# A fused decoder block on one core: the moving operand of the 512 column products read as two interleaved runs, and the banks emptied in steps of two

## What is computed

```python
proj = x @ w_in                      # (1024, 1024) @ (1024, 6656)
q, k, v, cb, cc, ch, g_conv, g_attn = split(proj)
y_conv = cb * causal_conv3(cc * ch)
y_attn = sliding_window_attention(q, k, v, sinks)     # window 128, 16 query heads, 4 kv heads, ALiBi
merged = sigmoid(g_conv) * y_conv + sigmoid(g_attn) * y_attn
x = layer_norm(ALPHA * x + merged @ w_out, ln1)
hid = silu(x @ w_gate) * (x @ w_up)                   # 1024 -> 2816
x = layer_norm(ALPHA * x + hid @ w_down, ln2)
```

## Time and profile before

| | |
|---|---|
| median of 3 runs | 1456.26 us (1455.56 to 1458.51) |
| profiled execution, its own time | 1455.48 us |
| its span, first to last instruction | 1453.6 us |
| TensorE busy | 1436.0 us, 99% |
| VectorE busy | 796.9 us, 55% |
| GpSimd busy | 601.7 us, 41% |
| ScalarE busy | 485.3 us, 33% |
| mean granted TensorE clock | 0.998 |

### The profile page before, as it was taken

How to read it: one execution, slowest core, us unless ns; L and a number is a source line. 1 busy time by engine, 2 the same in 40 slices (tenths; PEclk the granted TensorE clock), 3 DMA queues, 4 the chain that set the end, 5 groups by cost and what they waited for, 6 DMA issues and landing times. The chain is left out here.

```text
span 1453.6 us, 19033 instructions
## 1 busy us (share of the span) xinstructions
PE 1436.0 (99%) x6658; PEld 1193.9 (82%) x6658; DVE 796.9 (55%) x1196; ACT 485.3 (33%) x933; POOL 601.7 (41%) x374
## 2 busy tenths in 40 slices
PE   9999999999999999999999999999999999999997
PEld 8888888888888888887887788888888888888886
DVE  3126664566357743767867835535345453454547
ACT  4433433333234423434245332322323223232133
POOL 2212122212212131124873483754737547464464
PEclk9999999999999999999999999999999999999999
DMA  5211111111111011111420121112111112121112
GB/s 174 59 44 44 41 33 55 32 43 43 43 43 43 29 44 46 41 44 59 121 83 15 58 74 44 58 44 65 51 42 58 51 58 65 29 64 59 44 51 116
DMA packets 128406, 80.22 MB, mean 55 GB/s; under 512 B 8432, under 2 KB 123120, under 8 KB 128368
## 3 DMA queue, kind: packets, MB, share of 16 engines
q1 hardware_dynamic: 128368, 79.73, 18.2%
HBM read 75.53 MB, written 4.19 MB: 55 GB/s over the span
## 5 line engine op out<-in xcount | busy, mean ns | idle before, releaser
L476 POOL TENSOR_TENSOR w_lo<-raw,w_hi 128x1024 fp32r<-128x1024 f32 x54 | 131.7, 2439 | 507.2 <-ACT w_hi L616 507.2
L1353 PE MATMUL ps<-act_hi,w_hi 128*128 128x512 f32 x864 | 338.6, 392 | 1.2 <-DVE act_lo L913 1.2
L1355 PE MATMUL ps<-act_hi,w_lo 128*128 128x512 f32 x864 | 336.6, 390 | 0.0
L1354 PE MATMUL ps<-act_lo,w_hi 128*128 128x512 f32 x864 | 336.5, 390 | 0.0
L564 POOL TENSOR_TENSOR w_lo<-raw,w_hi 128x512 fp32r<-128x512 f32 x80 | 108.5, 1356 | 227.7 <-ACT w_hi L826 227.7
L1355 PEld LDWEIGHTS ps<-act_hi,w_lo 128*128 128x128 f32 x864 | 162.2, 188 | 34.4
L1353 PEld LDWEIGHTS ps<-act_hi,w_hi 128*128 128x128 f32 x864 | 162.3, 188 | 33.5 <-issue 1.4
L1354 PEld LDWEIGHTS ps<-act_lo,w_hi 128*128 128x128 f32 x864 | 162.4, 188 | 32.0
L1353 PE MATMUL ps<-hid_hi,wd_hi 128*128 128x512 f32 x320 | 124.9, 390 | 3.4 <-DVE res L1192 3.4
L1198 DVE TENSOR_TENSOR res<-res,ps 128x512 f32<-128x512 f32 x128 | 87.9, 687 | 68.3 <-PE ps L1355 67.7
L1354 PE MATMUL ps<-hid_lo,wd_hi 128*128 128x512 f32 x320 | 124.5, 389 | 0.0
(11 more groups left out here) (193 smaller groups left out, 2548.0 us busy)
## 6 DMA issues: line engine op xcount, KB each, us to landing
raw<-in_w_in SPq DMA_DIRECT2D x52, 512.0 KB, 3.8
raw_d<-in_w_down SPq DMA_DIRECT2D x22, 512.0 KB, 3.3
raw<-in_w_gate SPq DMA_DIRECT2D x40, 256.0 KB, 2.9
raw<-in_w_up SPq DMA_DIRECT2D x40, 256.0 KB, 3.2
raw<-in_w_out SPq DMA_DIRECT2D x16, 512.0 KB, 3.6
xs<-in_x SPq DMA_DIRECT2D x8, 512.0 KB, 8.1
out<-rows SPq DMA_DIRECT2D x7, 512.0 KB, 2.6
raw_b<-in_w_gate SPq DMA_DIRECT2D x1, 512.0 KB, 5.3
```

Source lines behind the costliest of these rows:

```text
L476: pool.tensor_tensor(w_lo[:, slot], raw[:, slot], fp(w_hi[:, slot]), ALU.subtract).then_inc(w_lo_s, 1)
L1353: pe.matmul(bank, w_h(t), a_hi(t), start=(t == 0), stop=False)
L1354: pe.matmul(bank, w_h(t), a_lo(t), start=False, stop=False)
L1355: last = pe.matmul(bank, w_l(t), a_hi(t), start=False, stop=(t == tiles - 1))
```

## The change

Each product over half a tile of tokens now reads its moving operand through `folded`: element 0, element 256, element 1, element 257, and so on. That holds for the three matmuls of `product`, the three of `pair_product` and the product with v. The matmul still writes its bank in one run, so column 2b + a of the bank now belongs to token 256a + b. Whoever empties the bank reads it through `bank_of`: every second column (0, 2, 4, ...) for the first 256 tokens, then 1, 3, 5, ... for the others. The SBUF side of these instructions keeps its layout, and `tokens` only writes it as two runs of 256 so that shapes match. For the product with v, `o_ps` and `lo` are read in steps of two in the same way. No instruction is added, removed or moved on any engine, no semaphore and no transfer changes. The scores, transposes, statistics, last rows and all weight loads keep their patterns.

```diff
+        def folded(ap):
+            return ap.rearrange("p (a b) -> p b a", a=2)
+        def tokens(ap):
+            return ap.rearrange("p (a b) -> p a b", a=2)
+        def bank_of(b):
+            return ps[:, b, :].rearrange("p (b a) -> p a b", a=2)
...
-                        bank = ps[:, unit_bank(n), :]
+                        bank = bank_of(unit_bank(n))
...
-                            act.activation(tga[:, j, half(h)], bank, ACT.Tanh, scale=0.5).then_inc(ga_s, 1)
+                            act.activation(tokens(tga[:, j, half(h)]), bank, ACT.Tanh, scale=0.5).then_inc(ga_s, 1)
...
-                    o_ps = ps[0:HD, OUT, :].rearrange("p (j e q) -> p e j q", j=2, e=2)
-                    lo = o_lo[:].rearrange("p (j e q) -> p e j q", j=2, e=2)
+                    o_ps = ps[0:HD, OUT, :].rearrange("p (e q j) -> p e j q", j=2, e=2)
+                    lo = o_lo[:].rearrange("p (e q j) -> p e j q", j=2, e=2)
...
-                tile = res[:, m, half(h)]
+                tile, bank = tokens(res[:, m, half(h)]), bank_of(4 + v % 4)
...
-                    dve.tensor_tensor(tile, tile, ps[:, 4 + v % 4, :], ALU.add).then_inc(add_s, 1)
+                    dve.tensor_tensor(tile, tile, bank, ALU.add).then_inc(add_s, 1)
...
-                    pe.matmul(bank, w_h(t), a_hi(t), start=(t == 0), stop=False)
-                    pe.matmul(bank, w_h(t), a_lo(t), start=False, stop=False)
-                    last = pe.matmul(bank, w_l(t), a_hi(t), start=False, stop=(t == tiles - 1))
+                    hi, lo = folded(a_hi(t)), folded(a_lo(t))
+                    pe.matmul(bank, w_h(t), hi, start=(t == 0), stop=False)
+                    pe.matmul(bank, w_h(t), lo, start=False, stop=False)
+                    last = pe.matmul(bank, w_l(t), hi, start=False, stop=(t == tiles - 1))
...
-                                last = pe.matmul(ps[:, OUT, :], vs[:, n - 1 + kb, :], part[:, kb],
+                                last = pe.matmul(ps[:, OUT, :], vs[:, n - 1 + kb, :], folded(part[:, kb]),
...
-                    b_hi, b_lo = right(j, t)
+                    b_hi, b_lo = (folded(ap) for ap in right(j, t))
```

More of the change, by code:

```diff
@@ L631, in _ @@
                 act.wait_ge(unit_s, n + 1)
-                bank = ps[:, unit_bank(n + 1), :]
+                bank = bank_of(unit_bank(n + 1))
                 if t < 2:
@@ L635, in _ @@
                         act.wait_ge(v_turned, n - 1)
-                    act.activation(yc[:, half(n % 2)], bank, ACT.Copy).then_inc(v_copied, 1)
+                    act.activation(tokens(yc[:, half(n % 2)]), bank, ACT.Copy).then_inc(v_copied, 1)
                 else:
@@ L641, in _ @@
                         for to in range(2):
-                            act.activation(res[to * HD:(to + 1) * HD, 2 * (2 * j + e), half(h)],
-                                           bank[e * HD:(e + 1) * HD, :], ACT.Copy).then_inc(k_copied, 1)
+                            act.activation(tokens(res[to * HD:(to + 1) * HD, 2 * (2 * j + e), half(h)]),
+                                           bank[e * HD:(e + 1) * HD], ACT.Copy).then_inc(k_copied, 1)
                 if (t, h) in ((0, 1), (1, 1), (2, 1)):
@@ L668, in _ @@
                                 rows = slice(e * HD, (e + 1) * HD)
-                                act.activation(q_st[rows, 2 * j + e, half(h)], bank[rows, :],
+                                act.activation(tokens(q_st[rows, 2 * j + e, half(h)]), bank[rows],
                                                ACT.Copy).then_inc(q_hi_s, 1)
                         elif kind == "ga":
-                            act.activation(tga[:, j, half(h)], bank, ACT.Tanh, scale=0.5).then_inc(ga_s, 1)
+                            act.activation(tokens(tga[:, j, half(h)]), bank, ACT.Tanh, scale=0.5).then_inc(ga_s, 1)
                         elif kind == "cc":
@@ L675, in _ @@
                                 act.wait_ge(conv_s, k * 24 + 12)
-                            act.activation(ccs[:, half(h)], bank, ACT.Copy).then_inc(cc_s, 1)
+                            act.activation(tokens(ccs[:, half(h)]), bank, ACT.Copy).then_inc(cc_s, 1)
                         elif kind == "gc":
@@ L679, in _ @@
                                 act.wait_ge(conv_s, k * 24 + 10)
-                            act.activation(tgc[:, half(h)], bank, ACT.Tanh, scale=0.5).then_inc(gc_s, 1)
+                            act.activation(tokens(tgc[:, half(h)]), bank, ACT.Tanh, scale=0.5).then_inc(gc_s, 1)
                         if h == 1 and n < 2 * NT - 1:
@@ L966, in unit @@
                             dve.wait_ge(q_hi_s, k * 8 + (4 * j + 2 * h + 2))
-                            dve.tensor_tensor(q_st[other, 2 * j + e, cols], bank[rows, :],
-                                              fp(q_st[rows, 2 * j + e, cols]), ALU.subtract).then_inc(q_lo_s, 1)
+                            dve.tensor_tensor(tokens(q_st[other, 2 * j + e, cols]), bank[rows],
+                                              tokens(fp(q_st[rows, 2 * j + e, cols])), ALU.subtract).then_inc(q_lo_s, 1)
                     elif kind == "ch":
@@ L973, in unit @@
                         conv_done(j, 4 * h)
-                        dve.tensor_tensor(u_pad[:, 2 + h * HALF:2 + (h + 1) * HALF], bank, ccs[:, cols],
+                        dve.tensor_tensor(tokens(u_pad[:, 2 + h * HALF:2 + (h + 1) * HALF]), bank, tokens(ccs[:, cols]),
                                           ALU.mult).then_inc(conv_s, 1)
@@ L993, in unit @@
                         conv_done(j, 10 + h)
[L994 to L995 removed]
+                        dve.tensor_tensor(tokens(res[:, bass.ds(k * 2 + j, 1), cols].rearrange("p a s -> p (a s)")), bank,
+                                          tokens(yc[:, cols]), ALU.mult).then_inc(conv_s, 1)
                 def soft_done(n, step):
@@ L1121, in _ @@
                 dve.wait_ge(xsum_s, DT * 2 if h else 2 * m + 1)
-                dve.scalar_tensor_tensor(out=res[:, m, half(h)], in0=res[:, m, half(h)], scalar=ALPHA,
-                                         in1=ps[:, out_bank(v), :], op0=ALU.mult, op1=ALU.add).then_inc(res_s, 1)
+                tile = tokens(res[:, m, half(h)])
+                dve.scalar_tensor_tensor(out=tile, in0=tile, scalar=ALPHA,
+                                         in1=bank_of(out_bank(v)), op0=ALU.mult, op1=ALU.add).then_inc(res_s, 1)
                 if h == 0:
@@ L1139, in hidden_up @@
                     dve.wait_ge(hid_s, 3 * t + 3)
-                dve.scalar_tensor_tensor(out=u_st[:, t], in0=t_g[:, t], scalar=1.0, in1=ps[:, 2 * t, :],
+                dve.scalar_tensor_tensor(out=tokens(u_st[:, t]), in0=tokens(t_g[:, t]), scalar=1.0, in1=bank_of(2 * t),
                                          op0=ALU.add, op1=ALU.mult).then_inc(hid_s, 1)
@@ L1245, in low @@
                                              op1=ALU.subtract).then_inc(pair_s, 1)
-                u1, u2 = u_st[:, 0], u_st[:, 1]
-                x, y, z, w = (ps[:, b, :] for b in (BX, BY, BZ, BW))
+                u1, u2, up, gate = tokens(u_st[:, 0]), tokens(u_st[:, 1]), tokens(u3[:]), tokens(t_g[:, 0])
+                gate_b = tokens(t_g[:, 1])
+                x, y, z, w = (bank_of(b) for b in (BX, BY, BZ, BW))
                 product_done(SECOND_SUM)
```

26 lines of the change are left out of this document (13 added, 13 removed).

## The result

The changed kernel takes 1405.59 us in the median of 4 runs (1404.44 to 1405.68), the kernel before 1455.91 us. The ratio is 0.965 with a 95% interval of 0.9633 to 0.9666. The forecast was wrong in sign and far off in size: the rival with a chance of 0.08 (faster, 1,395 us) came nearest, and 1,405.6 lies outside the range of 1,445 to 2,730.

The account below looks back on a forecast made before the run. TensorE's matmul count times start distance was taken as the bound. The profiled 1,455.5 us plus 1,244 for slower reads less 8 of waits gave 2,691.5, forecast as 2,692 us with 0.8 us for the median; range 1,445 to 2,730.

Parts of the forecast that it names:

- faster: Rival, chance 0.08: interleaved reads avoid a collision with the weight load, up to 10.5 ns less per matmul, 1,395 us.
- What bounds the kernel: TensorE, busy 1,436.0 of 1,453.6 us: 5,832 affected matmuls at 0.227 us each, 1,324 us, 91% of the span.
- The read of the moving operand: In the 5,832 products on TensorE: two cycles per column instead of one, 213 ns more per matmul, 1,244 us in all.
- the lower end: Lower bound for a changed matmul: no extra cost, 0.227 us as now, if the feed can follow two runs at once.
- the fixed 13.7 ns: Part of each 227 ns matmul left after 512 columns at one cycle each.
- The upper end: Upper bound for a changed matmul: two cycles per column, from transposes of 110 ns for 128 columns, so 440 ns.
- The rule of the Trainium skill: SBUF is read in 16-byte lines needing two accesses in a row; by it, above 1,456 us by an unknown amount.
- The write and the read of the banks: Bank writes keep their order at no cost; bank reads in steps of two on VectorE and ScalarE taken as zero.
- What is given back: TensorE's waits for other engines shrink because slower products leave those engines early: 8 us returned.
- as fed before: Rival, chance 0.25: the array's feed keeps two places at once, matmuls stay unchanged, 1,456 us within 0.2%.
- Only a little slower: Rival, chance 0.17: bank reads cost double, 1,460 to 1,464 us, or a fifth of a cycle per column, 1,705.
- Much slower: Rival, chance 0.10: each fetch takes as long as four columns and serves one, 867 ns per matmul, 5,188 us.

Follow-up runs that it names:

- e5: Kernel before, moving operand read as one run in steps of two (0, 2, 4 up to 510, then 1, 3, 5), banks in one run: 2753.72 us.
- e3: Kernel before, moving operand read as two interleaved runs in pairs (0, 1, 256, 257, 2, 3), banks in one run: 2060.8 us, ratio 1.4141.
- e7: Kernel before, moving operand read as two interleaved runs, each in steps of two (0, 256, 2, 258), banks in one run: 1455.37 us.
- e8: Kernel before, each of the first 256 tokens read twice (0, 0, 1, 1), the second 256 left out: 1405.95 us.
- e9: Kernel before, moving operand read as four interleaved runs (0, 128, 256, 384, 1, 129), banks in one run: 1744.17 us.
- e10: Kernel before, moving operand interleaved close by (0, 4, 1, 5, 2, 6, 3, 7, then 8, 12): 1404.38 us.
- e6: Kernel before, moving operand read as two interleaved runs in blocks of four (0 to 3, 256 to 259, 4 to 7), banks in one run: 1583.52 us.
- e11: Kernel before, contiguous moving operand, each pair product taking only the first 64 columns of its weight tile and writing 64 partitions: 1461.92 us.
- e2: Changed kernel with the moving operand read in one run as before, banks still in steps of two: 1456.49 us, ratio 1.0001 to the kernel before.
- e4: Kernel before, moving operand read as two interleaved runs in blocks of 128 columns, banks in one run: 1456.28 us, ratio 0.9997.

## Why the prediction was wrong

**What bounds the kernel** was read rightly: number of matmuls by distance of their starts, 5,832 of them, 0.227 us each. All of the change in time comes through that product.

**The read of the moving operand** is the step that failed. "Between these two ends I take the upper", 440 ns, with 0.227 us as the lower end. Measured are 216 ns, below both ends. The reasoning behind the choice was that a read which uses each fetched neighbourhood for one column has to fetch more often. Taken stream by stream, e5 is such an order, and it takes 452 ns. But the reasoning was applied to the wrong sequence. Seen column by column the change leaves a neighbourhood each time, but e3, e5, e7 and e8 cannot be put in order by one sequence of columns; they can by two, the even and the odd columns. In each of these the change uses 16 bytes four times in a row, where the contiguous order uses them twice. The lower end, no cost, excluded a gain without a reason that a row gave; the text had one in hand, the fixed 13.7 ns, and gave it a chance of 0.08. For the same reason "200.00 of 200.00 us" of busy time was no sign that the feed had nothing to spare: the busy time contained that fixed part, and 10.8 ns of it went away.

**The upper end was misread as well.** The transposes start 110 ns apart, and the text took that for two cycles per column. Matmuls that read 128 contiguous columns for the scores start as far apart, in the kernel before:

```profile
95.52 0.28 PE L1445 MATMUL ps<-ks_lo,q_st 128*128 128x128 f32 x1
...
96.19 0.28 PE L1445 MATMUL ps<-ks_lo,q_st 128*128 128x128 f32 x1
```

These are 6 steps of 0.112 us. The 16 matmuls of one column that stand before the second stretch at the lower clock, in the kernel after, do too:

```profile
751.39 1.92 PE L1497 MATMUL ps<-mean_of,sq_acc 128*128 128x1 f32 x16 [0.48 <-DVE sq_acc L1094]
753.17 0.46 PE L1368 MATMUL ps<-act_hi,w_hi 128*128 128x512 f32 x1
```

1.78/16 = 0.111 us. So 0.11 us is what such a short matmul takes here whether it has 1 column or 128, and not a price per column. e5 comes within 12 ns of the 440, but the row that gave the 440 did not measure such a price, so that agreement is luck.

**The rule of the Trainium skill** that was cited (Advanced Engine Details and Errata, SBUF Cachelines: two accesses in a row per line of 16 bytes), read column by column, put the time above 1,456 us, and the measurement refutes that. Taken per stream it points the right way: one use per line 452 ns (e5; e3 and e9, which leave a line at every access but come back to it, 333 and 273), two 227 (before, e7), four 216 (change, e8, e10). The runs add that with two uses 11 ns per matmul remain, and that two do not always suffice (e6, 250 ns). That these 11 ns are fixed per matmul and not per column was not tested: the 256 contiguous columns of the earlier trace rows start 0.12 us apart, but that is close to the 0.11 us of the short matmuls.

**The rival "faster"** had the size (10.5 ns per matmul; 10.8 measured) but not the cause, so its nearness is luck. A collision with the weight load is not supported by e11, and e7, whose reads are spread like the change's, has no gain. Its comparison with the transposes rests on the misread 110 ns. Its objection, that something at a matmul's start would be the same whatever the order after it, was wrong. Its 1,395 us is 10.6 us too low, because it had nothing for the 13.1 us that were lost on the way.

**The write and the read of the banks** at no cost: right, shown by e2 within 0.1% and by 686 against 687 ns; only L1048 grew, by 34 ns.

**What is given back** had the sign of the main step and fell with it: the waits of TensorE did not shrink by 8 us, they grew from 9.2 to 16.0 us, and with the clock and the hidden waits in the pairs 13.1 us were lost.

**The rival "as fed before"** assumed what e7 and e4 show for other orders. **"Only a little slower"** is not the change either; e6 shows such a price, 23 ns, for another order. **"Much slower"** is in none of the fourteen runs; the worst order tried, e5, takes 452 ns.

## What to carry to other kernels

For products with 4-byte moving operands of 512 columns, write down the addresses of the even and of the odd columns apart. In the runs each list made four accesses in a row within 16 bytes when the pace was best; a plain contiguous read makes two, and costs 11 ns more per matmul. Whether the order also helps at other widths was not run. Orders that use each 16 bytes once per list, or jump to and fro within a list every one or two accesses, cost 10% to 100% more than the contiguous one, so an order has to be tried by the distance of the matmul starts. A gain on TensorE is paid out only in stages where it is the bound: count the matmuls by stage first, and look for the waits that come next. And before a row is used as a price per column, look for a row of the same engine with another number of columns.

## What was not expected of the hardware

- Two orders that read the same 512 columns, 0, 256, 1, 257 and 0, 1, 256, 257, take 216 and 333 ns.
- The cost of jumps within a stream is not a simple function of their number: 250 ns for runs of four, 273 for four single runs (283 in the heads), 333 for runs of two. The runs leave open why.
- VectorE and ScalarE read PSUM in steps of two float32 at full pace (686 and 597 ns for 512 columns, against 687 and 600 for neighbours).
- An idle stretch of 3 us on TensorE was followed by 3.4 us at the 1.2 GHz level (matmuls 0.43 us apart), and so cost 1.7 us more than itself. In another execution of the same kernel the same idle stretch was followed by the 2.4 GHz level.
- Matmuls of 1 column and of 128 columns start equally far apart, 0.11 us.
